# The first mixer's loop of 24 heads: another order for the compression, the units and the compressed branch

## The reference, cut to what matters

```python
proj = h @ w_in
qa, ka, va, qb, kcb, vcb, ksb, vsb, kwb, vwb, gb = jnp.split(proj, PROJ_SPLITS, axis=-1)
out_a = moba_attention(...)                   # 8 heads of 64, causal, biased softmax
# nsa_attention: 8 query heads, 2 groups of keys and values, three branches
blocks = raw[:, :, idx] + pos                 # 15 windows of 32 tokens, stride 16
compressed = jax.nn.silu(blocks.reshape(B, G, n_cmp, NSA_CMP_LEN * dh) @ w1) @ w2
out_b = gc[..., 0:1] * o_cmp + gc[..., 1:2] * o_slc + gc[..., 2:3] * o_win
out = jnp.concatenate([out_a, out_b]) @ w_out
```

## Time and profile before

| | us |
|---|---|
| median of three runs (lowest, highest) | 1670.52 (1668.26, 1670.56) |
| the profiled execution | 1672.64 |
| its span, first to last instruction | 1671.3 |
| PE busy in it | 1630.0 |
| DVE, ACT, POOL busy | 945.5, 785.8, 129.6 |

### The profile page before, as it was taken

How to read it: one execution, slowest core, us unless ns; L and a number is a source line. 1 busy time by engine, 2 the same in 40 slices (tenths; PEclk the granted TensorE clock), 3 DMA queues, 4 the chain that set the end, 5 groups by cost and what they waited for, 6 DMA issues and landing times. The chain is left out here.

```text
span 1671.3 us, 29837 instructions
## 1 busy us (share of the span) xinstructions
PE 1630.0 (98%) x13094; PEld 1497.0 (90%) x13094; DVE 945.5 (57%) x1202; ACT 785.8 (47%) x1044; POOL 129.6 (8%) x117
## 2 busy tenths in 40 slices
PE   7999999989999999999998999999999999999998
PEld 7999987778999999999997889999999998889997
DVE  6544462455644565455896576455745565574545
ACT  6444452444534454444664245444534455564443
POOL 0000020000000001000276201000020001001000
PEclk9999999969999999999999999999999999999999
DMA  7745452322655546554530046555555533345542
GB/s 278 275 177 179 179 201 77 126 76 98 243 194 181 181 167 214 178 198 177 181 127 4 21 176 235 178 191 186 202 194 182 184 149 140 140 177 203 197 177 76
DMA packets 40865, 280.67 MB, mean 168 GB/s; under 512 B 4794, under 2 KB 4794, under 8 KB 8864
## 3 DMA queue, kind: packets, MB, share of 16 engines
q1 hardware_dynamic: 39024, 272.40, 45.5%
q0 software_dynamic: 1712, 6.37, 1.1%
HBM read 277.14 MB, written 1.08 MB: 166 GB/s over the span
## 5 line engine op out<-in xcount | busy, mean ns | idle before, releaser
L231 PE MATMUL P<-xt,whi 128*128 128x256 f32 x5088 | 934.7, 285 | 4.4 <-ACT whi L205 1.6
L231 PEld LDWEIGHTS P<-xt,whi 128*128 128x128 f32 x5088 | 803.5, 193 | 19.0 <-issue 9.0
L231 PE MATMUL P<-xt,wlo 128*128 128x256 f32 x2544 | 703.1, 284 | 0.0
L219 DVE TENSOR_TENSOR wlo<-raw,whi 128x2048 fp32r<-128x2048 f32 x245 | 559.8, 2290 | 99.1 <-PE P L231 76.9
L205 ACT ACTIVATE whi<-raw 128x2048 fp32r<-128x2048 f32 x245 | 467.4, 1908 | 145.5 <-PE P L231 119.5
L231 PEld LDWEIGHTS P<-xt,wlo 128*128 128x128 f32 x2544 | 489.6, 192 | 0.0
L687 DVE TENSOR_TENSOR AR<-P,AR 128x256 f32<-128x256 f32 x114 | 48.4, 425 | 332.7 <-ACT AR L658 332.7
L658 ACT ACTIVATE AR<-P 128x256 f32<-128x256 f32 x114 | 43.8, 384 | 352.5 <-PE P L231 352.5
L231 PE MATMUL P<-whi,hh 128*128 128x512 f32 x504 | 197.9, 393 | 0.0
L231 PE MATMUL P<-wlo,hh 128*128 128x512 f32 x504 | 196.8, 390 | 0.0
L231 PE MATMUL P<-whi,hl 128*128 128x512 f32 x504 | 196.1, 389 | 0.0
(11 more groups left out here) (226 smaller groups left out, 919.0 us busy)
## 6 DMA issues: line engine op xcount, KB each, us to landing
raw<-ws SPq DMA_DIRECT2D x249, 1024.0 KB, 4.8
gb<-gains SPq DMA_DIRECT2D x14, 512.0 KB, 7.1
AR<-by_distance POOLq DMA_DIRECT2D x1, 3072.0 KB, 19.3
x<-x_in SPq DMA_DIRECT2D x2, 512.0 KB, 4.0
AR<-mem_in POOLq DMA_DIRECT2D x1, 1024.0 KB, 5.4
AR<-gains SPq DMA_DIRECT2D x2, 512.0 KB, 4.8
out<-x SPq DMA_DIRECT2D x2, 512.0 KB, 2.6
cs<-cst SPq DMA_DIRECT2D x1, 737.0 KB, 14.4
```

The costliest lines, as they stand in the source:

```text
L219: dve.e.tensor_tensor(k.wlo[n % NLO][:, :], k.raw[u % NRAW][:, :], k.whi[n % NHI][:, :].bitcast(F32), ALU.subtract).then_inc(*k.s_lo.inc(u))
L231: return pe.e.matmul(o, l, r, start=start, stop=stop, skip_group_check=True)
```

## The change

It reorders the first mixer's work; no product, copy or split is added or dropped.

- The compression's units come right behind unit 5, as units 6 to 9, in steps 2 to 5, into banks 4 and 5. The moba queries and keys become units 10 and 11, in steps 6 to 9. The values stay (12, 13, steps 10 to 13).
- On GpSimd X2 comes ahead of the doubled keys; on DVE the positions are added right behind the second leading unit (keys) and in step 1 (values).
- Before the loop ACT makes the high part of one unit fewer, and each after the read of the leading unit in place of before; DVE makes one low part fewer.
- The turn of the compressed is in step 7, its second product in 8 (both in banks 4 and 5), the scores in 11, the turns of the probabilities in 14 and 15, their sums in 16 (in banks 6 and 7), each ahead of the weights' product of the step. Its gated addition comes before that of the windowed branch, which DVE now does in two parts, in steps 18 and 19.
- Units 14 and 15 are cut finer and spread over steps 14 to 18 (`cols_part_tensor`): a quarter, two, one, two, two.
- The nsa output is turned in steps 19 and 20, and units 16 and 17 follow in quarters: 20, 21, 23, 24.
- Heads 0 to 7's sums no longer wait for QB's second half; those from head 8 wait for the compressed values to be read out of bank 4, those from head 16 for the compressed branch's addition.

```diff
 def compress_tensor(k, pe, s, half):
-    b, u = s, U_MIX + 8 + 2 * s + half
+    b, u = 4 + s, U_MIX + 6 + 2 * s + half
     w = k.raw[u % NRAW]
     pe.wait_ge(*k.s_raw[u % NRAW].after(u))
-    pe.wait_ge(*k.s_dv.after("bk", 3))
+    pe.wait_ge(*k.s_dv.after("bk", 2 * s + 1))
...
 def mixer_between_tensor(k, pe, i):
     U = U_MIX
     if i < 2:
-        cols_half_tensor(k, pe, U + 5, 7, i)
+        cols_half_tensor(k, pe, U + 5, 5, i)
     elif i < 6:
+        s = (i - 2) // 2
+        if s:
+            pe.wait_ge(*k.s_ev.after("qb", 1))
+        compress_tensor(k, pe, s, i % 2)
+    elif i < 10:
+        if i == 7:
+            for s in range(2):
+                compressed_tensor(k, pe, s)
+        if i == 8:
+            cmp_tensor(k, pe, 0)
+        n = (i - 6) // 2
+        pe.wait_ge(*k.s_ea.after("gate", n))
+        cols_half_tensor(k, pe, U + 10 + n, n, i % 2)
+    elif i < 14:
+        for n in range(2):
+            pe.wait_ge(*k.s_ea.after("qk", n))
+        if i == 11:
+            cmp_tensor(k, pe, 1)
+        moba_values_tensor(k, pe, (i - 10) // 2, i % 2)
+    elif i < 19:
+        if i < 16:
+            cmp_tensor(k, pe, i - 11)
+        if i == 16:
+            cmp_tensor(k, pe, 5)
+        n = int(i >= 17)
+        pe.wait_ge(*k.s_ea.after("va", n))
+        cols_part_tensor(k, pe, U + 14 + n, n, {14: [(0, 0)], 15: [(0, 1), (1, 0)], 16: [(1, 1)],
+                                                17: [(0, 0), (0, 1)], 18: [(1, 0), (1, 1)]}[i])
+    elif i < 21:
+        a = i - 19
+        turn_tensor(k, pe, "nsa", tiles(k.O), lambda a, g: [k.s_ev.after("o", 2, a)], ((a, 1),), (4 + a,))
+    if i in (20, 21):
+        pe.wait_ge(*k.s_xl.after("nsa", 0, 1))
+        for n in range(2):
+            pe.wait_ge(*k.s_ea.after("qk", 2 + n))
+        out_tensor(k, pe, U + 16, 2, True, 0, (i - 20,))
+    if i in (23, 24):
+        out_tensor(k, pe, U + 17, 3, False, 0, (i - 23,))
...
 def mixer_scalar(k, act):
         lead_scalar(k, act, "mx", U + n, n, k.mx_cross[n], 0.125 if n == 2 else 1.0)
-        hi_to(k, act, U + 4 + n)
+        hi_to(k, act, U + 3 + n)
...
+        if i == 5:
+            hi_to(k, act, U + 10)
+        if i == 6:
+            compress_scalar(k, act)
+        if i in (7, 8):
+            hi_to(k, act, U + i + 4)
+        if i == 7:
+            head_cols_out(U + 10, 0, k.QA[:, 0:2, :], 0.125, 0)
...
+        if i in (14, 15):
+            cmp_scalar(k, act, i - 11)
+            hi_to(k, act, U + i + 1)
...
+        if i == 19:
+            turn_scalar(k, act, "nsa", U + 15, ((0, 1),), (4,))
         if i == 20:
-            hi_to(k, act, U + 18)
-        if i == 23:
-            turn_scalar(k, act, "nsa", U + 15, ((0, 1), (1, 1)), (4, 5))
-            hi_to(k, act, U + 19)
+            turn_scalar(k, act, "nsa", None, ((1, 1),), (5,))
+        if i in (20, 22):
+            hi_to(k, act, U + 8 + i // 2)
...
 def mixer_vector(k, dve):
         lo_to(k, dve, U + 3 + n)
+        if n == 1:
+            blocks_vector(k, dve, 0)
...
-    lo_to(k, dve, U + 6)
     for i in range(26):
         k.mixer.vector(dve, i)
-        if i == 0:
-            lo_to(k, dve, U + 7)
-        if i == 2:
+        if i == 1:
+            blocks_vector(k, dve, 1)
             dve.wait_ge(*k.s_used.after(U + 5))
-            dve.e.tensor_scalar(k.QB[:, 2:4, :], to_tiles(k, 7), 0.125, None, ALU.mult).then_inc(*k.s_ev.inc("qb", 1))
+            dve.e.tensor_scalar(k.QB[:, 2:4, :], to_tiles(k, 5), 0.125, None, ALU.mult).then_inc(*k.s_ev.inc("qb", 1))
+        if i == 3:
+            compress_vector(k, dve, 0)
+        if i == 5:
+            lo_to(k, dve, U + 10)
+            compress_vector(k, dve, 1)
...
+        if i in (11, 13, 15, 17):
+            lo_to(k, dve, U + 13 + (i - 11) // 2)
...
         if i == 16:
+            cmp_vector(k, dve, 5)
+        if i in (18, 19):
+            normalise_vector(k, dve, 2, (i - 18,))
         if i in (19, 20):
-            lo_to(k, dve, U + i - 2)
+            turn_vector(k, dve, "nsa", ((i - 19, 1),), (i - 15,))
+        if i == 20:
+            lo_to(k, dve, U + 17)
+        if i == 22:
+            lo_to(k, dve, U + 18)
...
 def mixer_pool(k, pool):
     pool.e.dma_start(k.W2, k.w2[:, :]).then_inc(*k.s_w2.inc(by=16))
-    pool.wait_ge(*k.s_tt.after("mx", 1, 1))
+    pool.wait_ge(*k.s_tt.after("mx", 0, 1))
+    for s in range(2):
+        pool.e.dma_start(k.X2[64:128, s, 0, 0:255], k.KV[0:64, s, 1:256]).then_inc(*k.s_dup[4 + 2 * s].inc(by=16))
+        pool.e.dma_start(k.X2[0:64, s, 1, :], k.KV[64:128, s, :]).then_inc(*k.s_dup[5 + 2 * s].inc(by=16))
...
     for i, (dst, s) in enumerate(((k.KS2, 0), (k.KW2, 1))):
+        pool.wait_ge(*k.s_tt.after("mx", 1, s))
```

More of the change, by code:

```diff
@@ L1020, in compressed_tensor @@
 def compressed_tensor(k, pe, s):
-    b = 6 + s
-    pe.wait_ge(*k.s_ev.after("o", 1, s))
+    b = 4 + s
     pe.wait_ge(*k.s_ea.after("ht", s))
@@ L1051, in cmp_tensor @@
         pe.wait_ge(*k.s_ev.after("vc"))
+        pe.wait_ge(*k.s_ev.after("o", 1, 1))
         for h in range(8):
@@ L1060, in cmp_tensor @@
         for q in (2 * step - 6, 2 * step - 5):
-            b = 1 - q % 2
+            b = 7 - q % 2
             if q < 2:
-                pe.wait_ge(*k.s_ea.after("qk", 3 - q))
                 pe.wait_ge(*k.s_ev.after("cl", 1))
@@ L1124, in cmp_scalar @@
             act.wait_ge(*k.s_pe.after("ct", q))
-            act.e.activation(k.CT[0:15, q * 512:(q + 1) * 512], k.P[1 - q % 2][0:15, :], ACT.Copy).then_inc(*k.s_ea.inc("ct", q))
+            act.e.activation(k.CT[0:15, q * 512:(q + 1) * 512], k.P[7 - q % 2][0:15, :], ACT.Copy).then_inc(*k.s_ea.inc("ct", q))
 def add_gated(k, dve, which, a, bank, cf):
-    before = {2: ("o", 1, 1) if a == 0 else ("o", 2, 0), "c": ("o", 2, 1) if a == 0 else ("o", "c", 0)}[which]
+    before = {"c": ("o", 1, 1) if a == 0 else ("o", "c", 0), 2: ("o", "c", 1) if a == 0 else ("o", 2, 0)}[which]
     dve.wait_ge(*k.s_ev.after(*before))
@@ L1135, in add_gated, with normalise_vector @@
     dve.e.tensor_tensor(k.O[:, a, 512:1024], k.O[:, a, 512:1024], k.TM, ALU.add).then_inc(*k.s_ev.inc("o", which, a))
-def normalise_vector(k, dve, which):
+def normalise_vector(k, dve, which, of=(0, 1)):
     rd, last, sums = k.RD[:, 16 * which:16 * which + 16], MIXER_LAST[which], MIXER_SUMS[which]
     rv = rd.rearrange("p (h a) -> p a h", a=2)
-    dve.wait_ge(*k.s_ax.after("mixer", last))
-    dve.e.reciprocal(rd, k.DEN[:, 16 * which:16 * which + 16]).then_inc(*k.s_dv.inc("rd", which))
-    dve.wait_ge(*k.s_dv.after("rd", which))
-    if which:
-        dve.wait_ge(*k.s_ea.after("gate", 1))
-        dve.e.tensor_tensor(rv, rv, k.GTv[:, :, :, which], ALU.mult).then_inc(*k.s_dv.inc("rg", which))
-        dve.wait_ge(*k.s_dv.after("rg", which))
-    dve.wait_ge(*k.s_ap.after("mixer", last))
-    for a in range(2):
+    if 0 in of:
+        dve.wait_ge(*k.s_ax.after("mixer", last))
+        dve.e.reciprocal(rd, k.DEN[:, 16 * which:16 * which + 16]).then_inc(*k.s_dv.inc("rd", which))
+        dve.wait_ge(*k.s_dv.after("rd", which))
+        if which:
+            dve.wait_ge(*k.s_ea.after("gate", 1))
+            dve.e.tensor_tensor(rv, rv, k.GTv[:, :, :, which], ALU.mult).then_inc(*k.s_dv.inc("rg", which))
+            dve.wait_ge(*k.s_dv.after("rg", which))
+        dve.wait_ge(*k.s_ap.after("mixer", last))
+    for a in of:
         cf = rv[:, a, :].unsqueeze(2).to_broadcast([128, 8, 64])
@@ L1171, in moba_values_tensor, with cols_part_tensor @@
         last.then_inc(*k.s_used.inc(u))
+def cols_part_tensor(k, pe, u, b, parts):
+    wh, wl = weights(k, u)
+    pe.wait_ge(*k.s_lo.after(u))
+    for s, g in parts:
+        for c in range(4 * g, 4 * g + 4):
+            w = slice((s * 8 + c) * 128, (s * 8 + c) * 128 + 128)
+            last = mm3(pe, k.P[b][:, s * NT:(s + 1) * NT], wh[:, w], wl[:, w], k.xt[:, c, :, 0, :],
+                       k.xt[:, c, :, 1, :], c == 0, c == 7)
+    if parts[-1] == (1, 1):
+        last.then_inc(*k.s_used.inc(u))
 def mixer_between_tensor(k, pe, i):
@@ L1177, in mixer_between_tensor @@
     if i < 2:
-        cols_half_tensor(k, pe, U + 5, 7, i)
+        cols_half_tensor(k, pe, U + 5, 5, i)
     elif i < 6:
-        n = (i - 2) // 2
-        pe.wait_ge(*k.s_ea.after("gate", n))
-        cols_half_tensor(k, pe, U + 6 + n, n, i % 2)
+        s = (i - 2) // 2
+        if s:
+            pe.wait_ge(*k.s_ev.after("qb", 1))
+        compress_tensor(k, pe, s, i % 2)
     elif i < 10:
-        s = (i - 6) // 2
-        pe.wait_ge(*k.s_ea.after("qk", s))
-        compress_tensor(k, pe, s, i % 2)
-    elif i < 14:
-        for s in range(2):
-            pe.wait_ge(*k.s_ev.after("ht", s))
-        moba_values_tensor(k, pe, (i - 10) // 2, i % 2)
-        if i == 12:
+        if i == 7:
@@ L1222, in sums_need @@
     def sums_need(i):
+        if i < 8:
+            return [k.s_ev.after("vg", 1)]
         if i < 16:
-            return [k.s_ev.after("vg", 1), k.s_ev.after("qb", 1)]
```

(10 more changed lines are left out.)

87 lines of the change are left out of this document (29 added, 58 removed).

## The result

The changed kernel takes 1648.56 us in the median of four runs (1646.09 to 1649.80), beside 1670.54 for the kernel before on the same chip (1668.26 to 1670.76): ratio 0.987, 95% interval 0.9853 to 0.9887. That is 22.0 us faster. The forecast was 1650.0, the range 1643 to 1656.

The account below looks back on a forecast made before the run. TensorE, busy 98%, was held back by idle and low clock in the first mixer: 12.1 + 17.8 = 29.9 us. Less 3.3 new idle and 6.1 slow clock, 20.5 gained: 1652.1 profiled, 1650.0 median; range 1643 to 1656.

Parts of the forecast that it names:

- Lost before, 29.9 us: First mixer of the kernel before: 12.1 us of PE idle plus 17.8 us of slow clock, all to be won.
- Start, 0.5 (0 to 1.2): Steps 0 to 5: old wait and low clock go; new PE idle of 0.5 us, between 0 and 1.2.
- The rule on the shared port: Start: if VectorE's subtraction blocked GpSimd's transfer descriptors, X2 starts 1.8 us later, PE idles about 2 us: 1652.
- Steps 6 to 13, zero: Steps 6 to 13: no new idle, units 10 and 11 just in time; bound 1.34 + 1.4 us if either slips.
- Steps 14 to 18, covered: Steps 14 to 18: round trips with 1.34, 2.93 and 0.91 us of idle are covered by 12 or 24 matmuls.
- Steps 19 to 25, idle 2.8: Steps 19 to 25: new PE idle of 1.6 us for head 21's maxima, 0.95 for head 23's, 0.25 in two short waits.
- So I expect the clock to fall there, at about 347: Tail of the mixer: idle among small products makes the clock fall, costing 4 to 7.3 us, taken as 6.1.
- Its own signs: Trace after: scores 2 unwaited, full clock for 100 us, 15-row products halved, last sums about 364; wrong if clock falls twice.
- (a): Rival, chance 0.20: the clock holds to the mixer's end with the same idle; 1643.9 us, 1641.5 to 1646.
- (b): Rival, chance 0.15: a hand-over in steps 0 to 8 slips and the clock falls once more; 1652.8 to 1656.5 us.
- (c): Rival, chance 0.05: the clock falls near step 14 and no cut piece of a unit raises it; about 1681 us.
- (d): Rival, chance 0.04: X2 or raw units come late, start idle remains or grows, later gain is lost; 1668 to 1672 us.

Follow-up runs that it names:

- the early half alone: The kernel before with only steps 0 to 9, unit order, GpSimd's order and early splits as changed, steps 10 to 25 as before: 1664.96 us, ratio 0.9965.
- the changed kernel's second profile: The changed kernel run again, unedited, on the chip of another set: 1650.13 us, ratio 0.988.
- the padded kernels: Changed kernel with compressed sums over 128 rows, 113 of them zero: 1643.50 us, again 1645.79; with low parts moved and compressed scores cut too, 1645.10.
- the idle of 3.11: Changed kernel with compressed sums zero-padded to 128 rows, and unit 17's low part made twice in step 20: 1649.95 us, ratio 0.9879.
- the split: Changed kernel with the compressed sums in two halves, steps 15 and 16, a quarter of unit 14 between them: 1647.84 us, ratio 0.9863.

## Why the prediction was right, point by point

- **Lost before, 29.9 us: right for the profiled execution.** Every item of it is gone: no idle at 247, 318 or 348, no slow stretch at 250 or from 348 to 380. 29.9 less what is lost anew in the trace after, 4.4 (below), is 25.5; PE's mixer from first scores to last sums is 25.9 shorter (147.57 to 121.70). But it is the loss of one execution: three other profiles with the same 1.34 us of idle at step 14 kept the clock there, so the 1.4 at 318 was no fixed part of it.
- **Start, 0.5 (0 to 1.2): right.** 0.16 of idle, and the first scores 0.65 later. The low part of unit 5 was ready at 237.66 (said: 236.2 to 238.5), PE wanted it at 238.60 (said: 238.0); maxima at 239 and 243 as said. In the other profiles with the new start the first scores waited up to 0.66 us. X2 landed 6.7 to 6.8 us after each issue, inside the 4.6 to 8.3 of the earlier trace rows.
- **The rule on the shared port: its result (2 us of idle, 1652) didn't come.** The timeline of GpSimd after, and the landing of the transfers of line L1395 (the first and the third of X2's four; those of L1396 the same):

```profile
226.29 0.54 POOL L1395 DMA_DIRECT2D AR<-AR  x1 [20.67 <-DVE AR L496]
...
227.85 0.52 POOL L1396 DMA_DIRECT2D AR<-AR  x1
...
231.16 1.76 POOL L1404 COPY AR<-AR 64x256 f32<-64x256 f32 x1
```

```profile
DMA to landing us min/median/max: 6.7/6.8/6.8
```

  The subtraction ran from 225.92 to 228.20. The first transfer was issued 1.9 us before its end and the last 0.35, and both landed after 6.7 to 6.8; had the first waited for VectorE, it would have taken some 1.5 longer than the last. The copy at 231.16, begun inside the next subtraction, took 1.76 and ended just behind that one (232.65), where four copies clear of one took 0.39 to 0.41. So the rule of the Trainium skill, "SBUF — State Buffer", "SBUF: two separate sides", holds for the copies here and isn't seen for the transfers. For a VectorE operation with two SBUF inputs, as the subtraction is, that section of the Trainium skill names the lock only against a GpSimd operation that reads SBUF, as the copies do; the prediction's rival took it wider.
- **Steps 6 to 13, zero: right, and thin.** Unit 11's low part was ready 0.7 us before its turn, because compressed products stand ahead of it; without them (the early half alone) the bound that the prediction named (1.34 of idle and 1.4 of clock) came, as 0.90 and a fall of 3.4 us.
- **Steps 14 to 18, covered: right on idle, wrong on the clock.** No idle, but behind the compressed sums the clock was low for 6.67 us, which costs 6.67 x (1 - 1/1.84) = 3.0. This is the step that failed: "each fall comes right after a stretch where PE worked little" was taken as the only way to a fall. No row of the trace before could have shown the other one here: its sums over 15 rows start at 354.79, in a stretch that was low already.
- **Steps 19 to 25, idle 2.8: mis-sized.** 1.26 came: 0.76 + 0.19 + 0.16 + 0.15. Head 21's maxima were ready 7.0 us after the end of scores 20, not 7.9, and PE was back after 6.3 as said. VectorE did stand 0.59 and 1.07 us for ScalarE's halves of the two nsa turns, which the prediction had as the delay; the path was shorter all the same, and which of its terms was too long isn't shown. The 0.95 for head 23 came as 0.15 or 0.16.
- **"So I expect the clock to fall there, at about 347", 6.1: wrong in this profile.** It held. The idle it rested on was half of what was said; where it was made 3.11 the clock fell, and once at 0.78.
- **The sum.** Said 3.3 + 6.1 = 9.4 lost anew. Found 1.4 (the start's 0.16 with the tail's 1.26) + 3.0 = 4.4. From 29.9 that leaves 25.5, against 25.0 between the profiled executions. The trace itself adds up: 25.9 less 0.65 at the start and 0.2 behind the mixer is 25.0; the low stretch at 807 to 811, which the trace before lacks, is within these 0.2. So the forecast of the medians, 1650.0 for 1648.56, was closer than its terms, and that is luck: 5 us less was lost than said, and 3 us of the profiles' difference are not in the medians.
- **Its own signs.** The 15-row products take about half their time (7.09 to 3.78), and scores 2 don't wait. But the clock was to be 1.00 through the first 100 us of the mixer and fell after 88.6, and the last sums came at 359.5, nearer (a)'s 358 than the forecast's 364. In the changed kernel's second profile it fell twice in the mixer (at 297.2 and 324.5), which the prediction had named as a sign that it is wrong.
- **The rivals.** (a), the clock holds to the end, 1643.9, is half true: it held in the tail, and the padded kernels, where it holds in step 16 too, run at 1643.5 to 1645.8 (1649.95 with the idle of 3.11). (b), the fall at unit 11, is what the early half alone does. (c), pieces that don't restore the clock: in the change the one fall in the mixer ended after 6.67 us, within unit 14 and the steps around it. (d) is out.

Open: what decides, from one execution to the next, whether the clock falls behind the compressed scores, behind the 12-row products, at 1.34 or at 0.78 us of idle, and when it rises under small products.

## What to carry to other kernels

Before moving a block of work, look at what stands directly ahead of the reduction that the next product waits for: moving one subtraction by one step gave as much as reordering ten steps. Walk each queue past which a step is moved, GpSimd's too, since leaving that one as it was cost 5 to 7 us. And where many small products over few rows stand together, try padding the rows with zeros while the clock is high: it cost the engine nothing here, and in the four profiles with padding the clock didn't fall at these sums, though it still fell elsewhere.

## What the runs showed of the hardware that I had not expected

- The clock fell with PE busy. Low stretches of about 3 to 7 us without any idle time of PE in them or shortly before: 326.37 to 333.04 in the change (6.67 of 6.67 us busy at 0.50), between 296 and 303 in five of nine profiles, and behind 12 products over 12 rows in a later stage in seven of fourteen. The Trainium skill, "TensorE: Matmul & The Clock Gate", "HAM oscillation — how this bites in real kernels", tells of falls where PE waits between groups of products; the trace agrees for the 3.11 us of idle and shows this other way besides.
- At the compressed sums in one piece: over 15 rows, four falls of four; over 128 rows, none of five, zeros or not in the added rows, at nearly the same durations (4.49 and 4.35 us for 38 records).
- The clock stayed low with PE busy, too: the same sums over 128 rows, in 9 us of which 8.86 were busy, left it at 0.50. And in the same late stretch of the old order it rose under small products in two profiles, at 363.4 and 366.3, and in two only under a unit's, at 378.5 and 379.8.
- One and the same idle time lets the clock fall in some executions only: 1.34 or 1.35 us at step 14 of the old order in one of four, 0.76 to 0.80 in the tail of the new one in one of seven.
- How often it falls varies between executions of one kernel, and the mean granted clock of a kernel's runs goes with their time (0.999 at 1641.37 us, 0.995 at 1648.74, both padded); the changed kernel's eight runs spread over 4 us and those of the split over 10.
